# The first block's output projection in plain fp32, other buffers for the query chunks and the first gathered rows, and a new place for four steps of dot products

## The chip, the cores and the metric

The kernel runs on one core of a Trainium2 chip. The metric is the device time of one execution, in microseconds (us); the times given are the median of three runs and their lowest and highest. The profile is one execution, and its span is counted from the first to the last instruction. The engines are PE (matmuls; PEld is its weight load), DVE (vector), ACT (scalar activations), POOL (which issues the gathers here) and SP (which issues the plain loads). All of them run their own programs in order and wait for each other by semaphores.

## What is computed

A transformer block with a mixer (pooling and attention) and a PEER feed-forward layer, and behind it a second block (two kinds of attention, and a convolutional feed-forward layer). 256 tokens, width 1024, fp32. What the change touches is in the first block:

```
mod = c_act @ w_ada[l] + b_ada[l]
shift1, scale1, gate1, shift2, scale2, gate2 = jnp.split(mod, 6, axis=-1)
h = modulate(x, norm_mix_g[l], shift1, scale1)
proj = h @ w_in[l]
...
merged = g_pool * (pooled @ w_branch_pool[l]) + g_attn * (attn @ w_branch_attn[l])
x = x + gate1[:, None, :] * (merged @ w_out[l])
h2 = modulate(x, norm_ffn_g[l], shift2, scale2)
x = x + gate2[:, None, :] * peer_ffn(h2, peer_wq[l], peer_sub_keys[l], peer_u[l], peer_v[l])
```

`peer_ffn` picks, for each token and each of 8 heads, 16 of 16384 experts. The scores are `h2 @ w_q` against 2 x 128 keys per head; two rounds of top 16 give the indices. Each chosen expert has a row of 1024 numbers for a dot product with h2 and a row of 1024 numbers to be added with the weight `softmax * gelu(dot)`. That is 2 x 128 rows for each tile of 128 tokens, 256 gathers in all, of 128 x 2048 numbers (1 MiB) each.

## The kernel before

**Memory.** `ring` holds six slots of 128 x 4096 numbers. Slots 0 to 3 take weight chunks of 2 MiB; slots 4 and 5 of the ring hold eight "high parts" (below) of 128 x 1024 numbers. The chunk table also knows slots 4 and 5 for chunks, which are the first two 4096 columns of `util`; `util` holds the gates of the mixer in its columns 0 to 4095, `merged` in 4096 to 6143, and a low part (`lo_r`) in 6144 to 8191. In the gather stage every ring slot is two row buffers, named (slot, half).

**Split matmuls.** Most weights are used in two parts of a reduced fp32 format: ACT writes the high part (`split_high`, L498), DVE the rest (`split_low`, L873), in quarters of a chunk, and PE makes three passes (high x high, high x low, low x high). The output projection (`mixed`, L1630) does so too: 4 groups (2 tiles of tokens x 2 halves of the columns) of 8 x 3 matmuls of 128 x 512. For it ACT also splits `merged` (`xm high`, L639) and DVE its rest (L1069). A few matmuls, such as those with the gathered rows (L1761), are in plain fp32; each then stands in the trace as two instructions.

**The mixer.** SP loads the chunks in the order of `chunk_table`, each when what was in its slot has been read; a load that waits holds up all behind it. `ada` chunks are not used by PE: DVE multiplies the four parts of a chunk with a row and sums them (`ada(c)`, L884, 4 instructions of 128 x 1024), and the chunk's slot (slot 1 for the late ones) is free for the next `ada` chunk when that is done. The attention runs in a loop of 11 steps on PE, ACT and DVE alike. In a step i PE does the scores of head i (L1473), two quarters of the input projection (L1421, 48 matmuls), the turning of the probabilities of head i - 2 (L1481), the values of head i - 3 (L1492, L1493) and small pieces of the pooling branch (L1593, L1594, L1602); from step 7 it does `branch(0, z)` (L1572) in place of the input projection. DVE does the masks of head i (L931), the norms of head i - 1 (L915, L918), low parts, and in steps 0, 1, 3 and 5 `ada(8)` to `ada(11)`; in step 6 also the low parts of the pooling branch (`xp low`, L896), for which `branch(0, 0)` waits. ACT does the exponentials of head i behind the mask of head i.

**From the mixer to the gathers.** PE: `branch(1, z)`, then `mixed` for (tile 0, half 0), (0, 1), (1, 0), the turned rows of tile 0 (L1516), the queries and scores of head 0 for tile 0 (L1662, L1672), `mixed(1, 1)` (L1630), head 1's queries and tile 1's. DVE: `merge` of each quarter (L1065, L1067), the residual of each projected half (L962, L965), and the routing of head 0 in tile 0, in whose midst stands the residual of (tile 1, half 1). The routing ends with the indices (L1165), for which POOL waits to issue the first gather.

**The gathers.** `FIRST_BUFS` names the seven row buffers that are used first; `LATER_BUFS` adds five more at given rows, when the query chunks have been read. A buffer is free when PE has added its last row (event `rows`). Of two rows (later four, at the end one) DVE takes the dot products (L1237), ACT the gelu (L733) and the diagonals (L738), PE adds the rows (L1761). PE does the other queries in pieces between the rows (L1647). After the last row SP loads the second block's first chunks.

## Time and profile before

| | us |
|---|---|
| median of 3 runs (lowest to highest) | 1257.58 (1256.51 to 1258.30) |
| the profiled execution, its own time | 1258.39 |
| its span | 1256.6 |
| PE busy in the span | 1094.6 |
| DVE busy | 834.0 |
| ACT busy | 438.4 |
| DMA engines, q0 (gathers), share of the span | 51.5% |
| DMA engines, q1 (plain loads), share of the span | 24.6% |

The span falls into the mixer and projection (0 to about 231 us), the gathers (to about 890 us) and the second block. A row of a timeline gives the start, the length of the group of instructions, the engine, the line, what is written and read, the count, and in brackets how long the engine had been idle before and what ended that. Times between two rows are differences of their starts. PEclk is the granted clock of PE, where 1.00 is 2.4 GHz and 0.50 is 1.2 GHz.

### The profile page before, as it was taken

To read this page: it belongs to the slowest core of one execution; us is meant where nothing else is said; L and a number is where in the kernel's file an instruction comes from. 1 tells how busy PE (TensorE), PEld (TensorE's weight loads), DVE (VectorE), ACT (ScalarE), POOL (GpSimd) and SP (SyncE) were. 2 spreads that over 40 slices of the span, in tenths; PEclk is the share of its full clock that TensorE was granted. 3 is DMA by queue.
4 is the path that set the end of the run, shared out by engine and by line. 5 is a ranking of instruction groups with operands and counts; after the bars stand their busy time and mean duration, and the time that the engine had idled before them with its cause. 6 is when DMAs were issued, how large, how long until landed. Compare 5 with 4: busy or idle time off the path is not lost.

```text
span 1256.6 us, 13533 instructions
## 1 busy us (share of the span) xinstructions
PE 1094.6 (87%) x4970; PEld 734.5 (58%) x4970; DVE 834.0 (66%) x1903; ACT 438.4 (35%) x908; POOL 289.8 (23%) x260
## 2 busy tenths in 40 slices
PE   5998899699899986876887878878799989999997
PEld 3797787554454442332333333333498768999986
DVE  5696675667777778778888454545645455887753
ACT  3533373232323232212223111112535454666542
POOL 0000000235445343443554544543000000000000
PEclk8999899899999999988898998989899998999999
DMA  9977531899999999999999999999653412545540
GB/s 376 427 299 308 204 119 68 348 398 412 422 421 421 421 422 421 422 421 421 418 422 421 421 421 421 422 420 422 253 225 135 168 44 91 178 191 202 185 151 34
DMA packets 47878, 389.39 MB, mean 310 GB/s; under 512 B 5442, under 2 KB 5826, under 8 KB 7236
## 3 DMA queue, kind: packets, MB, share of 16 engines
q0 software_dynamic: 36864, 268.45, 51.5%
q1 hardware_dynamic: 10948, 120.07, 24.6%
q8 instruction: 40, 0.66, 0.2%
q14 instruction: 26, 0.21, 0.0%
HBM read 387.45 MB, written 1.05 MB: 309 GB/s over the span
## 4 chain that ended last, share of the span: by engine, by line
PE 49%; DMA 29%; DVE 15%; ACT 4%; issue 1%; POOL 1%; SPq 1%; DVEq 0%; POOLq 0%
DMA ring<-in_uv,idx 23%; PE ps L1761 16%; PE ps L1421 14%; DMA ring<-in_w_ada 5%; PE ps L1886 5%; DVE ring L1237 3%; DVE ring_r L873 2%; DVE ring L884 2%; PE ps L1817 2%; PE ps L1443 2%; PE ps L1473 2%; PE ps L1647 1%; PE ps L1630 1%; PE ps L1572 1%; POOL ring L482 1%
## 5 line engine op out<-in xcount | busy, mean ns | idle before, releaser
L1761 PE MATMUL ps<-ring,probT 128*128 128x512 f32 x1024 | 499.2, 634 | 112.6 <-ACT probT L738 112.5
L1237 DVE CUSTOM_DVE_ANT_0 ring<-h2t,ring 128x1024 f32<-128x1024 f32 x256 | 310.1, 1223 | 179.7 <-DMA ring<-in_uv,idx 179.1
L482 POOL DMA_INDIRECT ring<-in_uv,idx x256 | 289.6, 1131 | 580.5 <-PE ps L1761 315.5
L1761 PEld LDWEIGHTS ps<-ring,probT 128*128 128x128 f32 x1024 | 200.7, 202 | 360.3 <-issue 202.7
L1421 PE MATMUL ps<-util_r,ring_r 128*128 128x256 f32 x1312 | 220.9, 287 | 5.1 <-DVE util_r L1209 3.9
L873 DVE TENSOR_TENSOR ring_r<-ring,ring_r 128x1024 fp32r<-128x1024 f32 x142 | 167.8, 1220 | 58.2 <-ACT ring_r L498 58.2
L1421 PEld LDWEIGHTS ps<-util_r,ring_r 128*128 128x128 f32 x1312 | 185.4, 193 | 10.2 <-issue 7.1
L498 ACT ACTIVATE ring_r<-ring 128x1024 fp32r<-128x1024 f32 x142 | 143.0, 1049 | 49.4 <-DMA ring<-in_w_in 26.3
L733 ACT ACTIVATE prob<-prob 128x2 f32<-128x2 f32 (+2 forms) x94 | 19.2, 204 | 381.0 <-DVE prob L1237 380.7
L1421 PE MATMUL ps<-h_r,ring_r 128*128 128x256 f32 x704 | 125.4, 281 | 0.0
L738 ACT ACTIVATE probT<-ct,prob 128x128 f32<-128x128 f32 x256 | 85.1, 392 | 73.9 <-DVE prob L1243 73.7
L1421 PEld LDWEIGHTS ps<-h_r,ring_r 128*128 128x128 f32 x704 | 108.2, 189 | 0.1
L884 DVE CUSTOM_DVE_ANT_0 ring<-h2t,ring 128x1024 f32<-128x1024 f32 x44 | 51.3, 1221 | 19.8 <-DMA ring<-in_w_ada 19.4
L1886 PE MATMUL ps<-ring_r,util_r 128*128 128x512 f32 x176 | 50.1, 395 | 0.0
L508 ACT ACTIVATE prob<-prob,mx 128x128 f32<-128x128 f32 (+1 forms) x48 | 21.5, 448 | 59.9 <-DVE mx L931 59.9
L1647 PEld LDWEIGHTS ps<-h_sb,ring 128*128 128x128 f32 x128 | 24.8, 195 | 24.8 <-issue 24.0
L1886 PEld LDWEIGHTS ps<-ring_r,util_r 128*128 128x128 f32 x176 | 32.9, 187 | 8.0
L1647 PE MATMUL ps<-h_sb,ring 128*128 128x256 f32 x128 | 36.5, 386 | 0.0
L1443 PE MATMUL ps<-ring_r,util_r 128*128 128x256 f32 x288 | 34.9, 281 | 0.0
L1443 PEld LDWEIGHTS ps<-ring_r,util_r 128*128 128x128 f32 x288 | 34.1, 188 | 0.7 <-issue 0.7
L1572 PE MATMUL ps<-area_r,ring_r 128*128 128x256 f32 x192 | 26.0, 298 | 5.3 <-DVE area_r L896 3.9
L1243 DVE TENSOR_TENSOR prob<-prob 128x2 f32<-128x2 f32 (+2 forms) x94 | 14.5, 155 | 23.6 <-ACT prob L733 23.6
(213 smaller groups left out, 1037.8 us busy)
## 6 DMA issues: line engine op xcount, KB each, us to landing
ring<-in_w_in SPq DMA_DIRECT2D x13, 2048.0 KB, 12.3
ring<-in_w_up SPq DMA_DIRECT2D x11, 2048.0 KB, 7.7
ring<-in_w_ada SPq DMA_DIRECT2D x7, 2048.0 KB
ring<-in_w_down SPq DMA_DIRECT2D x6, 2048.0 KB, 7.8
ring<-in_w_ada SPq DMA_DIRECT2D x8, 1024.0 KB, 15.5
ring<-in_w_out SPq DMA_DIRECT2D x4, 2048.0 KB, 8.5
ring<-in_w_q SPq DMA_DIRECT2D x3, 2048.0 KB, 7.6
ring<-in_w_br SPq DMA_DIRECT2D x2, 2048.0 KB, 10.0
```

Of the source, the lines that this page charges most:

```text
L482: e.indirect_dma_start(out=row_buf[n], out_offset=None, in_=uv, in_offset=bass.IndirectOffsetOnAxis(ap=idx[:, tt, k:k + 1], axis=0)).then_inc(
L498: e.activation(hi, w, ACT.Copy).then_inc(*high.put(q))
L738: e.activation(diag[:, n % 8, :], ident, ACT.Copy, scale=wt[:, tt, n % 128:n % 128 + 1]).then_inc(*acted.put(("diag", n)))
L873: e.tensor_tensor(lo, w, hi.bitcast(F32), ALU.subtract).then_inc(*low.put(q))
L884: e.tensor_tensor_reduce(wv, crow, wv, 1.0, 0.0, ALU.mult, ALU.add, mod[:, 4 * c + j:4 * c + j + 1]).then_inc(*made.put(("ada", c, j)))
L1237: e.tensor_tensor_reduce(u, h2t[:, tt, :], u, 1.0, 0.0, ALU.mult, ALU.add, av[:, tt, n % 128:n % 128 + 1]).then_inc(*made.put(("dot", n)))
L1421: ins = e.matmul(o[:, jj * T:(jj + 1) * T], w[:, k, :], r[:, k, :], start=(k == 0 and n == 0), stop=(k == KD - 1 and n == 2))
L1443: ins = e.matmul(o, r[:, k, tt * P:(tt + 1) * P], w[:, k, :, :], start=(k == 0 and n == 0), stop=(k == KD - 1 and n == 2))
L1572: ins = e.matmul(o[:, jj * T:(jj + 1) * T], w[:, k, jj * P:(jj + 1) * P], x3[:, k, :], start=(jj == 0 and k == 0 and n == 0), stop=(jj == ...
L1647: ins = e.matmul(bank(("q", h))[:, jj * T:(jj + 1) * T], w[:, k, z * P:(z + 1) * P], h_sb[:, k, :], start=(k == 0), stop=(k == KD - 1))
L1761: ins = e.matmul(acc[half][:, :], diag[:, n % 8, :], row_buf[n][:, D + half * 512:D + (half + 1) * 512], start=(k == 0), stop=(k == 127))
L1886: ins = e.matmul(ps[where["down", tt, half]][:, :], h[:, k, tile[tt]], w[:, 0, HALF[half]], start=(k == 0 and n == 0), stop=(k == KF - 1 a ...
```

## The change

1. **Projection.** `mixed` reads `merged` and the chunks `out` as they are: 8 plain fp32 matmuls of 128 x 512 in a group where there were 24 of the split kind. The eight `split_high` and `split_low` of the `out` chunks and the four splits of `merged` (L639, L1069) are gone.
2. **Query chunks.** Chunk q1 loads into ring slot 4 and q2 into ring slot 5 (the buffers of high parts; new slot numbers 6 and 7), q3 into the lower part of `util`, where the gates were. In SP's queue q1 now stands ahead of q0. q1 waits for quarter 35 (the last of `branch(0, z)`), q2 for quarter 39 (the last of `branch(1, z)`), q3 for the last `merge`. Before, q1, q2 and q3 waited for projections, q1 and q3 for the last, with q2 behind q1 in the queue.
3. **Row buffers.** The first seven are halves of slots 0, 2, 1 and 3, and slots 4 and 5 come in later, at the same rows. The very last row buffers are now those of slot 4, not of slot 1. The scores lie in the upper part of `util`; the splitting of tile 0's rows for the second block, which uses the same part, moves from row 156 to 196 on PE, and accordingly on ACT and DVE.
4. **Dot products.** `ada(8)` to `ada(11)` stand in steps 0, 2, 4 and 6, and the sum with the bias (`mod2`) in step 7.

```
@@ -52,7 +52,7 @@
              ("in", 6, 3), ("ada", 8, 1), ("br", 0, 0), ("ada", 9, 1), ("in", 7, 2), ("ada", 10, 1), ("br", 1, 3),
-             ("ada", 11, 1), ("out", 0, 2), ("out", 1, 1), ("keys", 0, 0), ("q", 0, 3), ("q", 1, 1), ("q", 2, 2), ("q", 3, 5)]
+             ("ada", 11, 1), ("out", 0, 2), ("out", 1, 1), ("keys", 0, 0), ("q", 1, 6), ("q", 0, 3), ("q", 2, 7), ("q", 3, 4)]
     then = ([("in2", i) for i in range(6)] + [("out2", 0), ("out2", 1)]
@@ -67,8 +67,8 @@
 Q2 = QUARTER["in2", 0, 0]
-FIRST_BUFS = ((4, 0), (4, 1), (0, 1), (5, 0), (5, 1), (3, 0), (3, 1))
-LATER_BUFS = {26: ((1, 0), 3), 27: ((1, 1), 3), 58: ((2, 0), 5), 59: ((2, 1), 5), 93: ((0, 0), 7)}
+FIRST_BUFS = ((0, 1), (2, 0), (2, 1), (1, 0), (1, 1), (3, 0), (3, 1))
+LATER_BUFS = {26: ((4, 0), 3), 27: ((4, 1), 3), 58: ((5, 0), 5), 59: ((5, 1), 5), 93: ((0, 0), 7)}
 BATCHES = [(n, 2) for n in range(0, 96, 2)] + [(n, 4) for n in range(96, 248, 4)] + [(n, 1) for n in range(248, 256)]
@@ -252,6 +252,7 @@
         slots = [ring[:, i * SLOT:(i + 1) * SLOT] for i in range(NW)] + [util[:, 0:SLOT], util[:, SLOT:2 * SLOT]]
+        slots += [ring[:, i * SLOT:(i + 1) * SLOT] for i in (4, 5)]
         slots_r = [ring_r[:, i * SLOT:(i + 1) * SLOT] for i in range(NW)] + [util_r[:, 0:SLOT], util_r[:, SLOT:2 * SLOT]]
@@ -284,11 +285,10 @@
         merged = three(util, 4096, 8)
-        xm_hi = area_r[:, 2048:4096].rearrange("p (k t) -> p k t", k=KD)
         rope_of = {"q": (qT, yT), "k": (kT, small[:, :].rearrange("p (j t) -> p j t", j=4))}
...
         Q3 = area[:, 0:4096].rearrange("p (j t) -> p j t", j=16)
-        s_all = util[:, 0:4096].rearrange("p (z j n) -> p z j n", z=2, j=16)
+        s_all = util[:, 4096:8192].rearrange("p (z j n) -> p z j n", z=2, j=16)
         sidx = stat[:, 0:256].bitcast(U32)
@@ -331,7 +331,7 @@

-        loaded = [Mark(sem(f"s_chunk{i}"), 16) for i in range(NW + 2)]
+        loaded = [Mark(sem(f"s_chunk{i}"), 16) for i in range(NW + 4)]
         half_loaded = {n: Mark(sem(f"s_half{n[0]}{n[1]}"), 16) for n in (("ada", 0), ("ada", 2), ("in", 0), ("ada", 1), ("ada", 3))}
@@ -360,8 +360,6 @@
                 return ("tokens", 0, 1)
-            if kind == "out":
-                return ("mix1", 1, i)
             if (kind, i) in TOKEN_CHUNKS:
@@ -393,7 +391,7 @@
         beside_in = {0: (26, 27), 3: (28, 29), 4: (30, 31)}
-        beside_br = {5: (32, 33), 6: (34, 35), 7: (36, 37), 8: (38, 39), 9: (40,)}
+        beside_br = {5: (32, 33), 6: (34, 35), 7: (36, 37), 8: (38, 39), }
         beside1 = [("in", 4 + (u + 1) // 2, 2 * ((u + 1) % 2)) for u in range(7)]
@@ -405,8 +403,12 @@
                     sp.wait_ge(done, ("rows", last_rows[slot]))
+                elif (kind, i) == ("q", 1):
+                    sp.wait_ge(done, ("quarter", 35))
+                elif (kind, i) == ("q", 2):
+                    sp.wait_ge(done, ("quarter", 39))
                 elif (kind, i) == ("q", 3):
-                    sp.wait_ge(done, ("mix1", 1, 1))
+                    sp.wait_ge(made, ("merge", 3))
                 elif earlier:
@@ -478,7 +480,7 @@
                 else:
-                    pool.wait_ge(done, {4: ("mix1", 1, 0), 0: ("quarter", 35), 5: ("mix1", 1, 1)}[b[0]])
+                    pool.wait_ge(done, {0: ("quarter", 35), 2: ("mix1", 1, 0), 1: ("mix1", 1, 1)}[b[0]])
                 e.indirect_dma_start(out=row_buf[n], out_offset=None, in_=uv,
@@ -624,22 +626,13 @@
                         xy_high(k)
-            split_high(41, 42)
             xy_high(3)
-            split_high(43)
             sqrt_table(44)
...
                     *acted.put(("gate1", half)))
-            for z in range(4):
-                act.wait_ge(made, ("merge", z))
-                act.wait_ge(done, ("pv", 1, 7))
-                e.activation(xm_hi[:, 2 * z:2 * z + 2, :], merged[:, 2 * z:2 * z + 2, :], ACT.Copy).then_inc(
-                    *acted.put(("xm high", z)))
-                split_high(44 + z)
-
             def shifted(tt, k):
@@ -666,7 +659,7 @@
                 act.wait_ge(done, ("scores", h, tt))
-                e.activation(s_all[:, tt, 2 * h:2 * h + 2, :],
+                e.activation(s_all[:, 1 - tt, 2 * h:2 * h + 2, :],
                              bank(("scores", h, tt))[:, 0:T].rearrange("p (j n) -> p j n", j=2), ACT.Copy).then_inc(
@@ -723,7 +716,8 @@
                     row_root(3, 0)
-                if b0 == 164:
+                if b0 == 204:
+                    act.wait_ge(made, ("gw", 1, 7))
                     for half in range(2):
@@ -1038,13 +1032,13 @@
                 split_low(*beside_in.get(i, ()))
-                if i in (0, 1, 3, 5):
-                    ada({0: 8, 1: 9, 3: 10, 5: 11}[i])
                 if i == 10:
...
                     attended(1, i - 3)
-                if i == 6:
+                if i in (0, 2, 4, 6):
+                    ada(8 + i // 2)
+                if i == 7:
                     dve.wait_ge(made, ("ada", 11, 3))
@@ -1057,7 +1051,6 @@
             pool_gated(3)
-            split_low(*range(41, 44))
             for z in range(4):
@@ -1065,12 +1058,6 @@
                 e.tensor_tensor(m, m, g, ALU.add).then_inc(*made.put(("merge", z)))
-                dve.wait_ge(acted, ("xm high", z))
-                e.tensor_tensor(lo_r[:, 2 * z:2 * z + 2, :], m, xm_hi[:, 2 * z:2 * z + 2, :].bitcast(F32),
-                                ALU.subtract).then_inc(*made.put(("xm low", z)))
-                if z > 0:
-                    split_low(43 + z)
-            split_low(47)
             def shifted(tt):
@@ -1125,7 +1112,7 @@
                 dve.wait_ge(acted, ("scores", h0, tt) if h0 + nh <= 2 else ("scores", h0 + nh - 1))
-                yield from top16((*key, "s"), 2 * nh, sv, si, s_all[:, tt, 2 * h0:2 * (h0 + nh), :], z3)
+                yield from top16((*key, "s"), 2 * nh, sv, si, s_all[:, 1 - tt, 2 * h0:2 * (h0 + nh), :], z3)
                 dve.wait_ge(made, (*key, "s", "at2", 2 * nh - 1))
@@ -1226,7 +1213,7 @@
                     x3_again(0)
-                if b0 == 168:
+                if b0 == 208:
                     for half in range(2):
@@ -1618,17 +1605,13 @@
             def mixed(tt, half):
-                o = group(("mix1", tt, half))[:, :]
-                o4 = o.rearrange("p (q n) -> p q n", q=4)
-                a = NW * SLOT + (QUARTER["out", half, 0] % HI) * 1024
-                wh = ring_r[:, a:a + 4096].rearrange("p (q k n) -> p k q n", q=4, k=KD)
-                wl = slots_r[SLOT_OF["out", half]].rearrange("p (k n) -> p k n", k=KD)
-                wait_low(QUARTER["out", half, 3])
+
+                o = group(("mix1", tt, half))
+                w = slots[SLOT_OF["out", half]].rearrange("p (k n) -> p k n", k=KD)
+                pe.wait_ge(loaded[SLOT_OF["out", half]], ("out", half))
                 for k in range(KD):
-                    pe.wait_ge(made, ("xm low", k // 2))
-                    for n, (to, w, x3) in enumerate(((o4, wh, xm_hi), (o4, wh, lo_r), (o, wl, xm_hi))):
-                        ins = e.matmul(to, x3[:, k, tile[tt]], w[:, k], start=(k == 0 and n == 0),
-                                       stop=(k == KD - 1 and n == 2))
+                    pe.wait_ge(made, ("merge", k // 2))
+                    ins = e.matmul(o[:, :], merged[:, k, tile[tt]], w[:, k, :], start=(k == 0), stop=(k == KD - 1))
                 ins.then_inc(*done.put(("mix1", tt, half)))
@@ -1679,7 +1662,7 @@
                     for z in range(2):
-                        a = (2 * tt + z) * P
+                        a = (2 * (1 - tt) + z) * P
                         ins = e.matmul(o[:, a:a + P], Q3[:, 2 * h + z, tile[tt]], keys3[:, 2 * h + z, :], start=True,
@@ -1751,7 +1734,7 @@
                 tt, k = divmod(n, 128)
-                if n == 156:
+                if n == 196:
                     turned_x(3, 0)
```

DVE's queue in steps 1 and 2 of the attention loop; L931 (now L925) is the mask of a head, L915 and L918 (L909 and L912) are its norm, L884 (L878) is one of the four dot products of `ada(9)`. Before:

```order
L915 RECIPROCAL mx<-mx 128x2 [waits s_act]
L918 TENSOR_SCALAR prob<-prob,mx 128x128 [waits s_dve]
L918 TENSOR_SCALAR prob<-prob,mx 128x256
L884 ISA ring,mod<-h2t,ring 128x1024 [waits s_chunk1]
L884 ISA mod 128x1
```

After:

```order
L912 TENSOR_SCALAR prob<-prob,mx 128x256
L925 ISA prob,mx<-ps2,ct 128x128 [waits s_pe]
L925 ISA mx 128x1
L925 ISA prob,mx<-ps2,ct 128x256
L925 ISA mx 128x1
L909 RECIPROCAL mx<-mx 128x2 [waits s_act]
L912 TENSOR_SCALAR prob<-prob,mx 128x128 [waits s_dve]
L912 TENSOR_SCALAR prob<-prob,mx 128x256
L878 ISA ring,mod<-h2t,ring 128x1024 [waits s_chunk1]
```

The mask and the norm of the next head now stand ahead of the wait for the chunk, not behind it.

DVE's queue between the branches and the projection; L1065 and L1067 (now L1058 and L1060) are a `merge`, L1069 is the low part of `merged`, L873 a low part of an `out` chunk. Before:

```order
L873 TENSOR_TENSOR ring_r<-ring,ring_r 128x8x128 [waits s_high] x3
L1065 TENSOR_TENSOR util<-ps1,util 128x512 [waits s_pe]
L1067 TENSOR_TENSOR util<-util 128x512 [waits s_dve]
L1069 TENSOR_TENSOR util_r<-util,area_r 128x512 [waits s_act]
L1065 TENSOR_TENSOR util<-ps4,util 128x512 [waits s_pe]
L1067 TENSOR_TENSOR util<-util 128x512 [waits s_dve]
L1069 TENSOR_TENSOR util_r<-util,area_r 128x512 [waits s_act]
L873 TENSOR_TENSOR ring_r<-ring,ring_r 128x8x128 [waits s_high]
```

After:

```order
L1058 TENSOR_TENSOR util<-ps1,util 128x512 [waits s_pe]
L1060 TENSOR_TENSOR util<-util 128x512 [waits s_dve]
L1058 TENSOR_TENSOR util<-ps4,util 128x512 [waits s_pe]
L1060 TENSOR_TENSOR util<-util 128x512 [waits s_dve]
L1058 TENSOR_TENSOR util<-ps2,util 128x512 [waits s_pe]
```

Only the merges are left, and none of them waits for ACT.

SP's queue at the end of the mixer; in_w_out are the `out` chunks, in_keysT the keys, in_w_q the query chunks. Before:

```order
L413 DMA ring<-in_w_out 128x4096 [waits s_dve]
L413 DMA ring<-in_keysT 128x2048 [waits s_pe]
L413 DMA ring<-in_w_q 128x4096 [waits s_pe] x2
L413 DMA ring<-in_w_q 128x4096
L413 DMA util<-in_w_q 128x4096
```

After:

```order
L415 DMA ring<-in_w_out 128x4096 [waits s_dve]
L415 DMA ring<-in_keysT 128x2048 [waits s_pe]
L415 DMA ring<-in_w_q 128x4096
L415 DMA ring<-in_w_q 128x4096 [waits s_pe]
L415 DMA ring<-in_w_q 128x4096
L415 DMA util<-in_w_q 128x4096 [waits s_dve]
```

The first query chunk behind the keys is now q1 and has no wait left of its own; the next is q0, which waits for PE as before; q2 follows it without another wait, and q3 waits for DVE's last merge, no longer for PE's last projection.

## Rows read from the trace of the kernel before

**Rows 1.** The page, section 4: the chain that ended last, its shares by line.

```profile
DMA ring<-in_uv,idx 23%; PE ps L1761 16%; PE ps L1421 14%; DMA ring<-in_w_ada 5%; PE ps L1886 5%; DVE ring L1237 3%; DVE ring_r L873 2%; DVE ring L884 2%; PE ps L1817 2%; PE ps L1443 2%; PE ps L1473 2%; PE ps L1647 1%; PE ps L1630 1%; PE ps L1572 1%; POOL ring L482 1%
```

**Rows 2.** Stretches of the trace: busy us of each engine, PEclk, DMA share, GB/s.

```profile
200.00:210.00 10.00, 9.88 (x42) 7.98 (x43) 3.32 (x8) 1.74 (x5) 0.00 (x0) 1.00 0.01 2
...
500.00:600.00 100.00, 78.45 (x157) 32.00 (x158) 81.72 (x233) 22.91 (x64) 42.41 (x37) 0.90 1.01 421
```

**Rows 3.** Timeline of PE in the attention loop (columns as told above).

```profile
111.17 5.94 PE L1421 MATMUL ps<-util_r,ring_r 128*128 128x256 f32 x48
121.78 0.88 PE L1481 MATMUL ps<-ct,prob 128*128 128x128 f32 x3 [4.67 <-ACT prob L508]
...
128.06 7.45 PE L1421 MATMUL ps<-util_r,ring_r 128*128 128x256 f32 x48
...
138.04 5.95 PE L1421 MATMUL ps<-util_r,ring_r 128*128 128x256 f32 x48
...
145.89 5.94 PE L1421 MATMUL ps<-util_r,ring_r 128*128 128x256 f32 x48
...
157.68 5.09 PE L1572 MATMUL ps<-area_r,ring_r 128*128 128x256 f32 x24 [3.87 <-DVE area_r L896]
```

**Rows 4.** Timeline of DVE in the same loop.

```profile
115.74 1.23 DVE L884 CUSTOM_DVE_ANT_0 ring<-h2t,ring 128x1024 f32<-128x1024 f32 x1 [7.33 <-DMA ring<-in_w_ada]
...
128.21 1.23 DVE L884 CUSTOM_DVE_ANT_0 ring<-h2t,ring 128x1024 f32<-128x1024 f32 x1 [0.38 <-DMA ring<-in_w_ada]
...
148.41 1.23 DVE L884 CUSTOM_DVE_ANT_0 ring<-h2t,ring 128x1024 f32<-128x1024 f32 x1 [7.38 <-DMA ring<-in_w_ada]
...
157.12 1.42 DVE L896 TENSOR_TENSOR area_r<-area,area_r 128x256 fp32r<-128x256 f32 x4
```

**Rows 5.** Timeline of SP: the issue of plain loads.

```profile
120.44 0.33 SPq L413 DMA_DIRECT2D ring<-in_w_ada  x1
135.54 0.33 SPq L413 DMA_DIRECT2D ring<-in_w_br  x1
135.91 0.62 SPq L413 DMA_DIRECT2D ring<-in_w_ada  x1
...
224.75 0.43 SPq L413 DMA_DIRECT2D util<-in_w_q  x1
```

**Rows 6.** Timeline of PE, the first and the next piece behind three projected groups.

```profile
190.76 0.39 PE L1630 MATMUL ps<-ring_r,area_r 128*128 128x512 f32 x1
...
211.43 1.95 PE L1516 MATMUL ps<-prob,x_sb 128*128 128x128 f32 x16
```

**Rows 7.** The chain in order of time: start, us, what.

```profile
218.27 5.62 PE ps L1630 x24
...
278.35 1.72 PE ps L1761 x4
```

**Rows 8.** Timeline of POOL: the issue of gather 0 and of gather 11.

```profile
231.09 1.07 POOL L482 DMA_INDIRECT ring<-in_uv,idx  x1 [230.64 <-DVE idx L1165]
...
264.40 0.94 POOL L482 DMA_INDIRECT ring<-in_uv,idx  x1 [1.68 <-PE ps L1761]
```

**Rows 9.** Timeline of DVE: dot products of rows 1, 11 and 255.

```profile
246.73 1.23 DVE L1237 CUSTOM_DVE_ANT_0 ring<-h2t,ring 128x1024 f32<-128x1024 f32 x1 [2.30 <-DMA ring<-in_uv,idx]
...
271.98 1.23 DVE L1237 CUSTOM_DVE_ANT_0 ring<-h2t,ring 128x1024 f32<-128x1024 f32 x1 [1.25 <-DMA ring<-in_uv,idx]
...
888.13 1.23 DVE L1237 CUSTOM_DVE_ANT_0 ring<-h2t,ring 128x1024 f32<-128x1024 f32 x1 [0.80 <-DMA ring<-in_uv,idx]
```

**Rows 10.** Timeline of SP behind the last row: the second block's first loads.

```profile
892.34 2.04 SPq L413 DMA_DIRECT2D ring<-in_w_in  x4
```

**Rows 11.** Timeline of ACT: the first high parts of the second block.

```profile
900.20 2.00 ACT L498 ACTIVATE ring_r<-ring 128x1024 fp32r<-128x1024 f32 x2 [4.87 <-DMA ring<-in_w_in]
```

**Rows 12.** Timeline of PE at the same place.

```profile
895.96 3.68 PE L1747 MATMUL ps<-prob,area 128*128 128x128 f32 x16 [3.70 <-DVE mx L989]
903.56 8.66 PE L1421 MATMUL ps<-util_r,ring_r 128*128 128x256 f32 x48 [3.92 <-DVE util_r L1209]
```

## The prediction, made before the changed kernel had run

> **What bounds the kernel now.** I read the page's chain first. Its largest share, 23% of the span, is the landing of gathered rows [rows 1]. The table of stretches then shows which limit that is: from 500 to 600 us the DMA engines are full (1.01) and move 421 GB/s [rows 2]. 256 gathers of 1.05 MB are 268.4 MB, or 637 us at that rate, 2.49 each, more than any engine needs for a row. So the gather stage can hardly get shorter. The kernel ends at (issue of gather 0) + (what the DMA moves ahead of it) + 637 and stalls + (what follows the last row). I therefore read three places in the timelines: the way to gather 0, issued at 231.09 [rows 8], the first landings, and the way from the last dot product, 888.13 [rows 9], to the second block's first column at 903.56 [rows 12].
>
> On the way to gather 0 PE stands still twice: 4.67 us to 121.78 and 3.87 to 157.68 [rows 3]. Both times DVE had waited in a step's dot products for their chunk, 7.33 and 7.38 us [rows 4], with the next head's mask or the low parts of the pooling branch behind it. While the projection runs (200 to 210) the DMA is idle, share 0.01 [rows 2]; three query chunks of 2.1 MB go out only at its end, the last at 224.75 [rows 5], right ahead of gather 0.
>
> **The change, term by term.** The profiled execution took 1258.39, 0.8 above the median of the runs; I sum against it and take the same difference off the median. Times in the attention loop are before's scale.
>
> *Dot products.* `ada(9)` moves behind mask and norm of head 2, whose inputs are there. DVE then does them at 108.4 and waits for the same chunk to 115.74 as before, but PE has what it needs. Its column of step 3 ends at 111.17 + 5.9 = 117.1, and the 4.67 of waiting goes. So does the slow stretch behind it: the pieces from 121.78 to 128.06 took 6.3, and the 48 matmuls took 7.45 against 5.95 at full clock [rows 3], so 3.1 + 1.5 more. The next column starts at 117.1 + 3.2 = 120.3. From 128.06 to 138.04 is 10.0, less the 1.5 that the slow matmuls cost, 8.5: the column of step 5 starts at 128.8, that of step 6, 7.85 later (138.04 to 145.89), at 136.7. That is 9.2 ahead. DVE's low parts for steps 5 and 6 are done by my replay of the two queues at about 125 and 130, ahead of PE.
>
> `ada(10)` now starts behind the low parts of step 4, at 130.7 (its chunk, 7.8 on the way, landed at 128.21 [rows 4, 5]), and ends at 135.4. Then `ada(11)`'s chunk is issued, hardly earlier than before (135.91). But the `br` chunk that SP issued 0.4 ahead of it [rows 5] waited for PE's column of step 4 and now goes at 126.2; alone the `ada` chunk takes 7.8, not 12.5, and lands at 143.2. DVE reaches it behind the copy of head 3's values, at 142.6 (end of PE's column) and 1.5 for pieces and copy, 144.1. Four instructions of 1.23 [rows 4] end at 149.0 at the latest; PE's first branch starts 0.56 behind the start of L896 (157.68 and 157.12), at 149.5 instead of 157.68: **8.2 earlier**. The stall of 4 us stays, now behind `ada(11)` itself. Everything to the end of the branches follows PE at the same distance. `mod2` one step later delays nobody: its reader on PE is 20 us off.
>
> *Projection.* Before, the first three groups run from 190.76 to 211.43, 20.7 us [rows 6], though one such group alone takes 5.62 [rows 7]: 3.8 are waits for splits. In plain fp32 a group is 16 instructions; four such, with the same 128 x 512 shape, take 1.72 [rows 7], so 6.88 a group and 20.6 for three: **0.0**. The merges cover it: the last is ready about 1.5 behind the start, and its columns are read 5 behind it. The fourth group costs 6.88 - 5.62 = **1.2**, and DVE waits for it in the midst of the routing, ahead of the indices. The dropped splits on ACT and DVE had been the cause of those 3.8 and are worth nothing more.
>
> The trace shows 16 fp32 instructions at 6.88 against 24 split ones at 5.62, a factor of 1.22 [rows 7]. The Trainium skill, in FP8 and Floating Point Precision, section TensorE Precision Notes, counts four passes for a true fp32 matmul; against three for the split form this would be 4/3, an estimate of 7.5 a group, and 4.0 us on the path in place of 1.2. The row has the same shape in fp32, so I go by the row.
>
> *Query chunks.* q1 goes out when quarter 35 is done and q0, q2 and q3 at the end of the branches; all have landed 20 us before gather 0, in DMA time that was empty. PE's fp32 queries find q0 as before. SP has no other load behind them that matters. In before, gather 1 was used at 246.73; less 2.49 that is a first landing of 244.24, 13.15 behind the issue at 231.09 [rows 8, 9]. With an empty DMA it is at least 6.2: 1.07 on POOL, 2.49 of transfer, and what a lone chunk has beyond its transfer, 7.8 - 2.1/0.421 = 2.8, if 0.2 of this overlaps. It is at most 7.6, which gather 11 took with two others on the way, from 264.40 to 271.98 [rows 8, 9]. I take 6.6, near the lower end, since nothing is in front of it: **6.5 earlier** (5.5 to 6.9). Then the seven buffers cycle as before: row 0's end follows from the landing of row 1 in both, so the same 2.6 us behind, and the stalls until the sixth pair of buffers comes in are the same. PE, the pacer here, is as late relative to the landings.
>
> The Trainium skill, in DMA: Bandwidth & Descriptors, section Anatomy of one DMA, fits 2.0 us + bytes/436 GB/s to a DMA from GpSimd. For a gather that is an estimate of 4.4, and the sum would be 2.2 us lower. No row of before shows a gather that short.
>
> *After the last row.* The loads of the second block went out at 892.34, when PE had added row 255 in slot 1 [rows 10]; the first landed at 900.20 [rows 11] and its split let PE go at 903.56. Now slot 1's last row is 253, so SP is held by the landing of row 255 alone, 888.1. The chunk lands at 896.0, the split is done at 898.6 and the turned rows on PE, which end at 895.96 + 3.68 = 899.6 [rows 12], are last. PE goes on at 899.7: **3.9 earlier**, and the stall of 3.92 is gone. Its 48 matmuls took 8.66 there against 5.95 [rows 3, 12]; without the idle time up to 2.7 of that go. I take **1.5**, about the middle, since PE starts this place at the low clock anyhow.
>
> *Moved and hidden.* The split of tile 0's rows from row 156 to 196 (8 matmuls, two copies, two subtractions) stays beside a full DMA and is needed only after row 255; its new wait, for the last weights of the routing, was over some 30 rows before. Were it not hidden it would cost 3 us.
>
> Sum: 8.2 - 1.2 + 6.5 + 3.9 + 1.5 = 18.9. 1258.39 - 18.9 = 1239.5 for a profiled execution, **1238.7** for the median.
>
> **The rivals.** *The forecast*, 1235 to 1243, with each term within its bounds.
>
> *A stall in place of the one removed.* If `ada(11)`'s chunk lands no earlier than 148.41, the branches start at 148.4 + 4.9 + 0.6 = 153.9, 3.8 earlier and not 8.2: 1243.1. For it: its issue hardly moves. Against: the `br` chunk is out of its way by 9 us.
>
> *Buffers.* The DMA is empty sooner, and seven buffers do not keep it full if PE begins row 0 at half clock and stays there for three rows more; each costs 1.7 then: about 5 us, 1243.7. For it: PE idles ahead of row 0 in both. Against: it did so before too, for longer.
>
> *Slower.* The fp32 projection at 1.2 GHz. PE's stall ahead of the branches stays, and the granted clock has been down behind such stalls. Four groups at half clock take 27.5 more, which the merges can't hide: 1238.7 + 27.5 = 1266.2. It decides from where more than 70% of the projection runs at the low level (18.9 of 27.5). Against: the clock is 1.00 there now, 30 us behind the stall [rows 2], and PE has no gap between.
>
> *It doesn't do what it says.* If gathers were held by something other than the loads (the landing stays 13 us behind the issue) and the chunk behind the last row by the DMA, 10 us of the sum would go: 1249.
>
> **How the numbers follow.** Forecast 0.70, stall 0.12, buffers 0.09, not what it says 0.05 (0.01 of it with no gain that could be told), slower 0.03, faster than all of this 0.01. The likeliest is 1238.7. The range goes from 1234, all terms at their ends and the first landing still earlier, to 1247, stall and buffers together. It leaves out the last three. A difference under 0.2% (2.5 us) can't be told from none. Faster by more 0.96, within 0.01, slower by more 0.03.
>
> **What would show it.** Right: no idle PE between 117 and 121; an idle of 4 to 5 us ahead of the first branch, at 149 to 150; the last query chunk issued near 184; gather 0 issued near 224 and the first dot product within 8 us of it; the last dot product near 875; the second block's loads issued within 1 us of it, and no second wait of PE ahead of the first column. Wrong: three groups of the projection over 22 us; a DMA share under 0.95 anywhere in the first 60 us of the gathers for more than before; a first landing more than 9 us behind its issue.

## The result

The changed kernel takes **1240.18 us** (median of 4 runs, 1238.98 to 1245.5), the kernel before 1257.94 beside it (4 runs, 1256.51 to 1260.88). The ratio is 0.9864, 95% interval 0.983 to 0.9898: 12.8 to 21.4 us faster. 1238.7 was forecast, 1234 to 1247 as the range. The profiled execution took 1240.34, with a span of 1238.4.

The page of the changed kernel: its head and the chain by engine and by line, as [rows 1].

```profile
span 1238.4 us, 13445 instructions
...
PE 52%; DMA 29%; DVE 12%; ACT 4%; issue 1%; POOL 1%; SPq 0%; DVEq 0%; POOLq 0%
DMA ring<-in_uv,idx 25%; PE ps L1408 16%; PE ps L1744 16%; PE ps L1869 5%; DMA ring<-in_w_ada 4%; DVE ring L1224 3%; PE ps L1614 2%; PE ps L1800 2%; PE ps L1559 2%; PE ps L1460 2%; PE ps L1430 2%; DVE ring_r L867 2%; DVE ring L878 2%; PE ps L1630 1%; POOL ring L484 1%
```

The gathers are still the largest item and their stage has not become shorter; what lies ahead of it and behind it has. In the timelines below a row is: start, us, engine, line, operation, out and in, count, and in brackets the idle time ahead of it and what ended it. PE of the changed kernel in the attention loop, as [rows 3]:

```profile
110.62 5.95 PE L1408 MATMUL ps<-util_r,ring_r 128*128 128x256 f32 x48
119.76 5.95 PE L1408 MATMUL ps<-util_r,ring_r 128*128 128x256 f32 x48
128.24 5.95 PE L1408 MATMUL ps<-util_r,ring_r 128*128 128x256 f32 x48
136.09 5.95 PE L1408 MATMUL ps<-util_r,ring_r 128*128 128x256 f32 x48
...
148.68 5.46 PE L1559 MATMUL ps<-area_r,ring_r 128*128 128x256 f32 x24 [4.67 <-DVE area_r L890]
```

No idle time near 117, every column at full speed, and the second stall still there, with another cause. DVE shows which: the four instructions of `ada(11)` start at 143.54 and wait for no chunk, the low parts follow at 148.12.

```profile
143.54 1.21 DVE L878 CUSTOM_DVE_ANT_0 ring<-h2t,ring 128x1024 f32<-128x1024 f32 x1
...
148.12 1.42 DVE L890 TENSOR_TENSOR area_r<-area,area_r 128x256 fp32r<-128x256 f32 x4
```

The projection on PE (as [rows 6, 7]), the last query chunk on SP (as [rows 5]), gather 0 on POOL and the dot product of row 1 on DVE (as [rows 8, 9]):

```profile
182.17 20.76 PE L1614 MATMUL ps<-ring,util 128*128 128x512 f32 x48
...
209.44 7.03 PE L1614 MATMUL ps<-ring,util 128*128 128x512 f32 x16
...
183.81 0.33 SPq L415 DMA_DIRECT2D util<-in_w_q  x1
...
223.70 1.07 POOL L484 DMA_INDIRECT ring<-in_uv,idx  x1 [223.25 <-DVE idx L1152]
...
232.87 1.22 DVE L1224 CUSTOM_DVE_ANT_0 ring<-h2t,ring 128x1024 f32<-128x1024 f32 x1 [2.38 <-DMA ring<-in_uv,idx]
```

And the way out of the gathers, SP and PE (as [rows 10, 12]). The last dot product starts at 873.68, and SP no longer waits for PE:

```profile
873.67 2.06 SPq L415 DMA_DIRECT2D ring<-in_w_in  x4
...
881.51 3.48 PE L1730 MATMUL ps<-prob,area 128*128 128x128 f32 x16 [3.70 <-DVE mx L983]
885.09 5.92 PE L1408 MATMUL ps<-util_r,ring_r 128*128 128x256 f32 x48
890.86 2.90 PE L1777 MATMUL ps<-util_r,small_r 128*8 128x256 f32 x24
```

**Where 18.2 us of span went.** The execution is cut into pieces at the same instructions in both kernels. Both kernels were traced a second time (`before_again`, `after_again`, below), on two different chips; the last column is that pair. Each forecast is a term of the prediction's sum. Minus is time saved.

| piece | forecast | first pair | second pair |
|---|---|---|---|
| start to the column of step 2 | 0 | -0.55 | -0.50 |
| to the first branch (dot products) | -8.2 | -8.45 | -5.99 |
| to the start of the projection | 0 | +0.41 | -0.74 |
| to gather 0 (plain fp32) | +1.2 | +1.20 | +1.20 |
| to the dot product of row 1 (query chunks) | -6.5 | -6.47 | -6.67 |
| to the dot product of row 255 | 0 | -0.59 | +0.79 |
| to the second block's first column | -3.9 | -4.02 | -4.20 |
| its 48 matmuls (clock) | -1.5 | -2.73 | -1.00 |
| to the end | 0 | +3.00 | -0.79 |
| sum | -18.9 | -18.20 | -17.90 |

The last piece of the first pair is the surprise: 3.0 us of what had been won is given back some 100 us behind the change. The two rows are stretches of the changed kernel in the attention of the second block (busy us of PE, PEld, DVE, ACT, POOL, then PEclk, DMA share, GB/s):

```profile
988.00:992.00 4.00, 3.50 (x11) 2.17 (x11) 2.43 (x9) 2.87 (x8) 0.00 (x0) 0.50 0.00 0
992.00:996.00 4.00, 4.00 (x10) 2.81 (x9) 2.73 (x9) 2.81 (x8) 0.00 (x0) 0.50 0.02 4
```

PE runs at the lower of its two levels (1.2 GHz) there, behind several short waits (0.4 to 0.8 us each, from 982 on). Whether the change did that, or chance, is asked below, under `after_again`.

### The profile page after: what moved, and what is told of

Same layout as the page of the kernel before. It is cut to its first block, busy times and chain, and to the rows that moved or that the text cites. A ratio compares the mean times of both kernels' runs of the same rounds, so it can differ in the third digit from the quotient of the medians.

```text
span 1238.4 us, 13445 instructions
## 1 busy us (share of the span) xinstructions
PE 1092.4 (88%) x4938; PEld 723.5 (58%) x4938; DVE 821.9 (66%) x1891; ACT 428.2 (35%) x896; POOL 292.4 (24%) x260
## 4 chain that ended last, share of the span: by engine, by line
PE 52%; DMA 29%; DVE 12%; ACT 4%; issue 1%; POOL 1%; SPq 0%; DVEq 0%; POOLq 0%
DMA ring<-in_uv,idx 25%; PE ps L1408 16%; PE ps L1744 16%; PE ps L1869 5%; DMA ring<-in_w_ada 4%; DVE ring L1224 3%; PE ps L1614 2%; PE ps L1800 2%; PE ps L1559 2%; PE ps L1460 2%; PE ps L1430 2%; DVE ring_r L867 2%; DVE ring L878 2%; PE ps L1630 1%; POOL ring L484 1%
## 5 line engine op out<-in xcount | busy, mean ns | idle before, releaser
L1408 PE MATMUL ps<-util_r,ring_r 128*128 128x256 f32 x1312 | 216.6, 282 | 2.3 <-DVE ring_r L867 2.2
L867 DVE TENSOR_TENSOR ring_r<-ring,ring_r 128x1024 fp32r<-128x1024 f32 x134 | 158.3, 1220 | 54.7 <-ACT ring_r L500 54.7
L1408 PEld LDWEIGHTS ps<-util_r,ring_r 128*128 128x128 f32 x1312 | 181.0, 188 | 7.0 <-issue 3.9
L500 ACT ACTIVATE ring_r<-ring 128x1024 fp32r<-128x1024 f32 x134 | 134.6, 1049 | 46.5 <-DMA ring<-in_w_in 23.4
L878 DVE CUSTOM_DVE_ANT_0 ring<-h2t,ring 128x1024 f32<-128x1024 f32 x44 | 51.2, 1219 | 9.6 <-DMA ring<-in_w_ada 9.4
```

The costliest lines, as they stand in the source:

```text
L500: e.activation(hi, w, ACT.Copy).then_inc(*high.put(q))
L867: e.tensor_tensor(lo, w, hi.bitcast(F32), ALU.subtract).then_inc(*low.put(q))
L878: e.tensor_tensor_reduce(wv, crow, wv, 1.0, 0.0, ALU.mult, ALU.add, mod[:, 4 * c + j:4 * c + j + 1]).then_inc(*made.put(("ada", c, j)))
L1408: ins = e.matmul(o[:, jj * T:(jj + 1) * T], w[:, k, :], r[:, k, :], start=(k == 0 and n == 0), stop=(k == KD - 1 and n == 2))
```

## The experiments

Eleven runs were made: eight edited kernels, one of them twice, and the two kernels of the comparison once more each. Times are medians with the ratio to the kernel before, which ran beside them, and its 95% interval. They fall into three groups, each on a chip of its own: `e1` to `e4`, with 1257.65 for the kernel before (20 runs); `e5`, `e6`, `e7` and `after_again`, with 1258.31 (7); `e7_again`, `e8` and `before_again`, with 1257.04 (9).

### Dot products alone (`e1`)

The kernel before, with this edit on DVE:

```
-                if i in (0, 1, 3, 5):
-                    ada({0: 8, 1: 9, 3: 10, 5: 11}[i])
...
+                if i in (0, 2, 4, 6):
+                    ada(8 + i // 2)
-                if i == 6:
+                if i == 7:
```

> The kernel before with one edit: ada(8) to ada(11) in steps 0, 2, 4 and 6, the sum with the bias in step 7. Theory (the dot products on DVE hold PE, and all that follows moves with PE): the idle of 4.67 us ahead of 121.78 goes, the first branch on PE starts near 149 instead of 157.68, gather 0 is issued near 223 instead of 231.09, and the median falls by 8.2 from 1257.9 to 1249.7. Rival (the gain needs the other parts, because the splits of the output weights or the query chunks then set gather 0): gather 0 stays within 3 us of 231.09, the median is above 1255. The tail behind the last row is untouched in both: 3.9 of idle ahead of the second block's first column.

Measured: 1252.12 us (10 runs), 0.9959 (0.994 to 0.9978). PE and POOL of this kernel:

```profile
148.90 5.46 PE L1572 MATMUL ps<-area_r,ring_r 128*128 128x256 f32 x24 [4.68 <-DVE area_r L896]
...
222.78 1.07 POOL L482 DMA_INDIRECT ring<-in_uv,idx  x1 [222.34 <-DVE idx L1165]
```

Both landmarks are where the theory put them (149, 223), so the gain needs no other part of the change. But by the ratio the time fell by 5.2 (2.8 to 7.5), not by 8.2. From the column of step 2 to the first branch this trace takes 46.18; the kernel before took 54.65 in its first trace, but the kernel of `e2`, whose loop is before's, took 52.44. The second trace of before, further down, shows what differs.

### Plain projection alone (`e2`)

The kernel before, with `mixed` as in the changed kernel and the splits for it gone:

```
-            split_high(41, 42)
...
-            split_high(43)
...
-                act.wait_ge(made, ("merge", z))
...
-            split_low(*range(41, 44))
...
-                dve.wait_ge(acted, ("xm high", z))
...
-                    pe.wait_ge(made, ("xm low", k // 2))
+                    pe.wait_ge(made, ("merge", k // 2))
+                    ins = e.matmul(o[:, :], merged[:, k, tile[tt]], w[:, k, :], start=(k == 0), stop=(k == KD - 1))
```

> The kernel before with one edit: the projection in plain fp32 from the unsplit chunks, no splits of them and none of merged. Theory (a plain group costs 1.25 more than a split one on PE, the 3.8 of waits in the first three groups covered that): three groups in 20.6 us, the fourth in 6.9, the median 1.2 up, 1259.1. Rival (the splits on ACT and DVE were a cost of their own, which goes): gather 0 earlier than 231.09 by up to 3.8, the median 1254 to 1257.

Measured: 1261.31 us (10 runs), 1.0023 (1.0006 to 1.004). PE and POOL:

```profile
189.43 20.76 PE L1612 MATMUL ps<-ring,util 128*128 128x512 f32 x48
...
216.70 7.03 PE L1612 MATMUL ps<-ring,util 128*128 128x512 f32 x16
...
230.95 1.07 POOL L482 DMA_INDIRECT ring<-in_uv,idx  x1 [230.50 <-DVE idx L1150]
```

From the start of the projection to gather 0 it is 41.52 us; before 231.09 - 190.76 = 40.33, and 40.32 with the dot products moved alone. So plain fp32 costs **1.20 us** on the way to gather 0, and the many splits that it saves on ACT and DVE are worth nothing there. The time rose by more, 2.9 by the ratio, but the interval (0.8 to 5.0) holds the 1.20. In the trace the landing of row 1 (0.8) and the second block's first column (1.1) come later too, and the mean granted clock of the ten executions is 0.944, against 0.950 in the twenty of before. Whether plain fp32 brings any of that, no run shows. By itself this part of the change is a loss; it pays by what it frees, the buffers of the high parts, into which the query chunks can go early.

### Query chunks late (`e3`)

The changed kernel, with q0 first in SP's queue again and the others behind the last projected group:

```
-             ("ada", 11, 1), ("out", 0, 2), ("out", 1, 1), ("keys", 0, 0), ("q", 1, 6), ("q", 0, 3), ("q", 2, 7), ("q", 3, 4)]
+             ("ada", 11, 1), ("out", 0, 2), ("out", 1, 1), ("keys", 0, 0), ("q", 0, 3), ("q", 1, 6), ("q", 2, 7), ("q", 3, 4)]
...
                 elif (kind, i) == ("q", 1):
-                    sp.wait_ge(done, ("quarter", 35))
-                elif (kind, i) == ("q", 2):
-                    sp.wait_ge(done, ("quarter", 39))
-                elif (kind, i) == ("q", 3):
-                    sp.wait_ge(made, ("merge", 3))
+                    sp.wait_ge(done, ("mix1", 1, 1))
```

> The changed kernel with one edit: q1, q2 and q3 go out only when the last projected group is done, into their new buffers. Theory (6.3 MB of query chunks ahead of the first gathers is what delayed the first landing in before): gather 0 is issued as in the changed kernel, near 223.7; row 1's dot product starts 15 us behind the issue instead of 9.2, and the median is 6.5 up, 1246.7. Rival (the first landing depends on something else, the buffers' places or the clock): row 1's dot product within 10 us of the issue, the median 1240 to 1242.

Measured: 1247.21 us (5 runs), 0.9925 (0.99 to 0.9951), 7.0 above the changed kernel. The dot products of rows 0 and 1, behind a gather 0 issued at 223.01:

```profile
235.62 1.23 DVE L1220 CUSTOM_DVE_ANT_0 ring<-h2t,ring 128x1024 f32<-128x1024 f32 x1 [7.33 <-DMA ring<-in_uv,idx]
...
239.56 1.23 DVE L1220 CUSTOM_DVE_ANT_0 ring<-h2t,ring 128x1024 f32<-128x1024 f32 x1 [2.70 <-DMA ring<-in_uv,idx]
```

Row 1 comes 16.55 behind the issue, against 9.17 in the changed kernel, and row 255 is 7.7 later (881.35 against 873.68). The queue of chunks ahead of the first gather is the cause of that part.

### Second loads late (`e4`)

The changed kernel, with one more wait of SP ahead of the second block's loads:

```
             sp.wait_ge(arrived[255], 255)
+            sp.wait_ge(done, ("rows", 255))
```

> The changed kernel with one edit: SP sends the second block's loads only when PE has added row 255, as before the change. Both theories: the loads go out 4.2 later, near 877.9, PE waits a second time ahead of the first column and runs it at the low clock (8.7 instead of 5.9 us), so the 24 matmuls behind it start 6.6 later. Theory 1 (the cost of the tail is paid to the end): the median is 6.6 up, 1246.8. Theory 2 (the half-clock stretches of the attention behind it, at 988 to 997 and 1035 to 1041, are there because this one is missing; they cost 4.2 us more than before's, of which 1.2 comes back at 1042): they shrink again and 3.0 of the 6.6 comes back, 1243.8.

Measured: 1245.17 us (4 runs), 0.991 (0.9878 to 0.9942), 5.0 above the changed kernel. SP and PE:

```profile
878.34 1.97 SPq L415 DMA_DIRECT2D ring<-in_w_in  x4
...
889.39 8.60 PE L1409 MATMUL ps<-util_r,ring_r 128*128 128x256 f32 x48 [3.86 <-DVE util_r L1197]
897.82 2.96 PE L1778 MATMUL ps<-util_r,small_r 128*8 128x256 f32 x24
```

The second wait and the slow column are back, and the median lies between those of the two theories. Set to the last dot product, the 24 matmuls start 23.70 behind it (897.82 - 874.12) and 17.18 in the changed kernel: 6.5 us, as both theories said. Against the first trace of the changed kernel these matmuls start 6.96 later (897.82 - 890.86), and at the end of the span only 4.0 us of that remain, which is what theory 2 said. But this is no proof of it, as the next run shows.

### The changed kernel once more (`after_again`)

> The changed kernel once more, unedited, on this chip, for a second trace. Theory (from the first matmuls of the second block to the end of its attention an execution takes 143.4 us, or 2.3 to 3.3 more where the granted clock falls in the attention; which of the two, no kernel decides): this stretch, from the 24 matmuls behind the first column to the second LayerNorm's rows, is at 143.4 or between 145.5 and 147. Rival (the change itself brings the fall of the clock at 988 to 997, since the earlier one behind the first column is gone): it is above 145.5 again. The landmarks up to the last dot product repeat within 0.7 us of the first trace. Median 1240 to 1242.

Measured: 1240.35 us (4 runs), 0.9861 (0.9839 to 0.9884). The landmarks repeat less well than expected: row 255 is within 0.3 us, but gather 0 (222.74) is 1.0 and row 1 (231.74) 1.1 earlier than in the first trace. From the 24 matmuls to the second LayerNorm's rows it took 144.42 us, where the first trace has 146.70: neither at 143.4 nor between 145.5 and 147, so the two levels that the theory named are not two. From the 24 matmuls to the end of the span the thirteen traces have 344.5 to 347.5. The kernels with the long wait in the tail have 344.5 and 346.5 (before), 346.5 (`e1`), 347.3 (`e2`) and 344.6 (`e4`); those without it 347.5 and 345.7 (the changed kernel), 344.6 (`e3`), 346.9, 345.4, 345.4, 347.5 and 344.6 (`e5` to `e8`). The spread inside either group is as wide as that between them. That the change brings the fall of the clock is not borne out; that 3 us come and go there from one execution to the next is.

### The kernel before once more (`before_again`)

> The kernel before once more, for a second trace of its attention loop. Theory (after PE's idle of 4.67 us at 121.78 the granted clock falls in some executions only, and in those the loop is 2.2 us longer): either as in the first trace, 48 matmuls at 128.06 in 7.45 us and the first branch at 157.7, or as in e2_plain_alone, 5.94 us and the first branch at 155.5. Rival (the clock falls there always, and e2's earlier branch has another cause): 7.45 and 157.7 again.

Measured: 1256.8 us (one run). PE in the attention loop, as [rows 3]:

```profile
121.47 0.87 PE L1481 MATMUL ps<-ct,prob 128*128 128x128 f32 x3 [4.74 <-ACT prob L508]
...
127.11 5.95 PE L1421 MATMUL ps<-util_r,ring_r 128*128 128x256 f32 x48
...
154.82 5.46 PE L1572 MATMUL ps<-area_r,ring_r 128*128 128x256 f32 x24 [3.47 <-DVE area_r L896]
```

The same stall as in the first trace, but the branch 2.86 earlier (2.48 set to the column of step 2). The stretches behind the stall, first of the first trace, then of this one (PEclk is the third number from the end):

```profile
121.00:125.00 4.00, 3.22 (x9) 2.08 (x10) 1.77 (x10) 4.00 (x14) 0.00 (x0) 0.53 0.91 291
125.00:129.00 4.00, 4.00 (x13) 2.63 (x12) 3.15 (x3) 2.41 (x5) 0.00 (x0) 0.50 0.55 233
129.00:133.00 4.00, 4.00 (x27) 4.00 (x26) 4.00 (x9) 0.00 (x0) 0.00 (x0) 0.69 0.01 2
```

```profile
121.00:125.00 4.00, 3.53 (x11) 2.33 (x12) 1.50 (x9) 4.00 (x12) 0.00 (x0) 0.50 1.00 348
125.00:129.00 4.00, 4.00 (x24) 3.02 (x24) 3.49 (x3) 2.10 (x5) 0.00 (x0) 0.83 0.41 176
129.00:133.00 4.00, 4.00 (x36) 4.00 (x35) 4.00 (x11) 0.20 (x1) 0.00 (x0) 1.00 0.03 6
```

So the theory needs mending: the clock falls behind the stall both times (0.53, 0.50), and what differs is how soon it is back, by some 5 us: a clock of 0.69 from 129 to 133 means the low level to about 131.5, one of 0.83 from 125 to 129 means to about 126.4. The dot products are worth 8.45 against the one trace and 5.99 against the other. `e1`'s 5.2 fits the second better, and `e2`'s loop, 52.44, was of the short kind too (52.17 here). That the short kind is the usual one, three traces don't show.

### The last dot products later (`e5`)

The changed kernel, with `ada(11)` one step later:

```
-                if i in (0, 2, 4, 6):
-                    ada(8 + i // 2)
+                if i in (0, 2, 4, 7):
+                    ada(8 + min(i, 6) // 2)
```

> The changed kernel with one edit: ada(11) in step 7, behind the mask and norm of head 7, and no longer in step 6 ahead of the low parts of the pooling branch. Theory (the 4.67 us for which PE stands ahead of its first branch are the four dot products of ada(11) alone, nothing is late behind them): the low parts start at 143.5 instead of 148.1, the first branch near 144.1 instead of 148.7, and it runs at full clock (3.1 instead of 5.5 us), since PE has not stood still: 4.6 to 6.9 earlier, median 1240.2 - 5.5 = 1234.7. Rival (another wait takes the place: the second output chunk, which is released later, or the splits of step 7 behind ada(11)): the projection starts less than 2 us earlier, median 1238 to 1242.

Measured: 1236.4 us (4 runs), 0.9835 (0.9807 to 0.9863). PE and POOL:

```profile
144.06 3.08 PE L1559 MATMUL ps<-area_r,ring_r 128*128 128x256 f32 x24
...
218.21 1.07 POOL L484 DMA_INDIRECT ring<-in_uv,idx  x1 [217.77 <-DVE idx L1152]
```

PE does not stand still at all ahead of its first branch, which also runs at full clock. Gather 0 is 5.5 earlier, row 255 6.0 (867.66), the median 3.8, less than the 4.6 to 6.9 that were expected. The stall that the prediction left in place "behind `ada(11)` itself" was four instructions in the wrong place. A small part of it comes back at the fourth branch:

```profile
156.40 0.55 PE L1468 MATMUL ps<-ct,prob 128*128 128x128 f32 x3 [0.96 <-DVE prob L912]
...
159.60 3.10 PE L1559 MATMUL ps<-area_r,ring_r 128*128 128x256 f32 x24 [1.86 <-DVE util L933]
```

PE waits for DVE, which is now later by the four instructions, for 0.96 + 1.86 = 2.82 us in step 9 and 10, where the changed kernel has one wait of 1.47. Here the clock stayed up; in `e7` and `e8`, which have the same edit, it did not.

### The indices first (`e6`)

The changed kernel, with this edit on DVE:

```
-            advance(routing, 8)
+            advance(routing, 14)
             rows_added(2, 1, (1,))
-            advance(routing, 2)
             row_part(2, 1)
-            advance(routing, 1)
             row_diagonal(2, 1)
-            advance(routing, 3)
             shifted(1)
```

> The changed kernel with one edit on DVE: the second half of tile 1's residual, its row sums and its diagonal stand behind the cast to the indices of head 0, not ahead of it. Theory (what a slower fourth projected group costs, it costs because DVE waits for it ahead of the indices): the wait of 2.48 and 1.9 us of work leave the way, gather 0 goes out at 219.3 instead of 223.7, the last dot product is 4.4 earlier, and the median is 1235.8. Rival (PE and DVE take the rows up no earlier, since PE's queries and tile 1's rows come later, and few buffers stall the gathers): gather 0 early, but the last dot product less than 2 us earlier, median 1238.5 to 1241.

Measured: 1239.07 us (4 runs), 0.9855 (0.9831 to 0.9878), not to be told from the changed kernel. POOL shows gather 0 where the theory had it, 0.6 early, and then what ate it:

```profile
218.66 1.07 POOL L484 DMA_INDIRECT ring<-in_uv,idx  x1 [218.22 <-DVE idx L1152]
...
223.76 0.94 POOL L484 DMA_INDIRECT ring<-in_uv,idx  x1 [0.30 <-issue]
231.34 1.63 POOL L484 DMA_INDIRECT ring<-in_uv,idx  x1 [6.63 <-PE ps L1642]
```

Five gathers go out, the sixth waits 6.63 us for PE's queries of tile 1 (L1642), whose chunk holds its buffer; in the changed kernel they ended earlier and it waited for nothing (POOL issued it at 230.06, 6.4 behind gather 0). DVE takes up row 0 only at 229.80. Row 255 is at 871.95, 1.7 earlier. The rival's numbers came, and its mechanism with them: most of an early gather 0 is lost again if the rows are taken up no sooner and the buffers behind it come later. Which of the two costs how much, this run doesn't part.

### Both (`e7`), and a milder form (`e8`)

> The changed kernel with the edits of the two runs before it together. If both hold, they lie behind one another on the same way to gather 0 and add up: gather 0 near 213.5 to 214.7, the median 10 below the changed kernel, 1230.3. If one of them only moves a wait, the sum is that of the other alone, 1235.

Measured: 1233.39 us (4 runs), 0.9798 (0.9771 to 0.9825), gather 0 at 215.79, 1.1 later than expected at the latest. The fourth branch, at the low clock, takes 1.5 more than in `e5`, which covers that lateness:

```profile
159.91 4.58 PE L1556 MATMUL ps<-area_r,ring_r 128*128 128x256 f32 x24 [1.86 <-DVE util L933]
```

The median is 6.8 below the changed kernel's, not 10, and row 255, at 870.08, even comes behind `e5`'s 867.66: the two edits don't add up in full. The sixth gather again waits 6.63 us for PE's queries, and row 1 is 0.9 behind `e5`'s; the other 1.6 lie between row 1 and row 255, a stretch that differs by 1.9 us from trace to trace anyway (below). `e8` takes twelve routing steps ahead of the residual and leaves two behind it (`advance(routing, 12)`, then one ahead of `row_diagonal` and one behind).

> The kernel of e5 (ada(11) in step 7) with a milder form of e6's edit: twelve steps of the routing instead of eight ahead of the second half of tile 1's residual, so that they fill DVE's wait of 2.48 us for the fourth projected group, and the rest of that work still ahead of the indices. Theory (e6 lost its 4.4 us because tile 1's queries, whose end frees the buffers of gathers 5 and 6, came 1.8 later, and the five gathers ahead of them had all landed): here the queries end as in e5, gather 0 goes out 2.0 us earlier than in e5 (216.2), gathers 5 and 6 follow without a pause, and the last dot product is at 865.7, 2.0 earlier than e5's 867.66. Rival (any earlier gather 0 is lost again, since PE takes up row 0 no sooner): last dot product at 867 to 868.

Measured: 1234.59 us (5 runs), 0.9821 (0.979 to 0.9853). From the end of the third projected group to gather 0 it is 18.87 us and 20.94 in `e5`, 2.1 less where 2.0 were expected, and row 1 keeps them (27.78 against 29.94), though the sixth gather waits 2.02 us for PE's queries and doesn't follow without a pause. By row 255 only 0.4 is left (670.03 against 670.39). The absolute times are those of `e5` (gather 0 at 218.16), since the fourth branch ran at the low clock, as in `e7` (24 matmuls in 4.62 in place of 3.10 us), and the whole trace was 0.5 later from step 2 on; row 255 is at 869.32, later than either theory had it. That gather 0 and row 1 move is seen, that it is worth anything at the end is not.

> The kernel of e7 once more, to set it against e8 in the same rounds. By the last dot product it should lose: 870.08 in its first trace, against 865.7 expected of e8. The medians then differ by 4 us, 1237 against 1233. Rival (what e7 loses in the gathers comes back behind them, as its first median of 1233.4 beside e5's 1236.4 says): medians within 1.5 us.

Measured: 1234.09 us (5 runs), 0.9806 (0.978 to 0.9832), row 255 at 870.79, the fourth branch once more slow (4.64 us). The medians of `e7` and `e8` are within 0.5 us of one another, as the rival said; that its reason is the right one isn't shown. `e5`, `e7` and `e8` can't be ranked by these runs; their medians are 3.8 to 6.8 us below the changed kernel's, and `e7`'s nine runs (1230.71 to 1237.43) lie below all eight of the changed kernel (1238.98 to 1245.5). So do the four of `e5` (1233.55 to 1238.69), by less; of the five of `e8` one doesn't (1240.24).

## Why the prediction was right, and where it was not

**The bound.** That the gather stage itself would not move held: from row 1 to row 255 641.40 before, 640.81 after (641.47 and 642.26 in the second pair; 640.3 to 642.3 over the thirteen traces).

**Dot products.** The replay of the loop was right to 0.8 us: the columns were forecast at 120.3, 128.8 and 136.7 and came at 119.76, 128.24 and 136.09, the branch at 149.5 and came at 148.68; 0.55 of that the run was ahead already. The step that was wrong is the one that took the slow matmuls behind the stall, "3.1 + 1.5 more", as a fixed part of the stall's price. In the second trace of before about 2.5 us of it aren't there. The difference between two medians holds an average of such draws, and the prediction had only one. The 8.45 of the first pair is near the forecast because both rest on the same trace of before.

**Projection.** 20.6 us for three groups and 6.87 for the fourth, forecast 20.6 and 6.88; 1.20 of cost against 1.2. The price came from the four matmuls of the same shape [rows 7]. From the four passes that the Trainium skill, in FP8 and Floating Point Precision, section TensorE Precision Notes, counts for a true fp32 matmul, the prediction had made an estimate of 7.5 a group; the runs stand with the row, 6.9. (The 4.0 us on the path that it gave for this case are 3.7 by its own figures.)

**Query chunks.** 6.47 against 6.5. Row 0's dot product starts 5.56 behind the issue, 0.28 after DVE began to wait, so the estimate of 4.4 that the prediction worked out from the Trainium skill, DMA: Bandwidth & Descriptors, section Anatomy of one DMA, is too short counted from the start of POOL's instruction. Counted from its end, 224.77, the way is 4.49, which is near it. The prediction's 6.6 was for row 1's dot product less one transfer, 6.68 as measured.

**After the last row.** 4.02 and 4.20 against 3.9. The clock term, set at 1.5 "about the middle", measured 2.73 and 1.00 in the two pairs; over the thirteen traces the column takes 7.3 to 8.7 us behind the long wait (five traces, mean 7.95) and 5.9 to 7.0 without it (eight, mean 6.26), so it is worth 1.7.

**What was missing.** The sum, 18.9, is near the 18.2 of the first pair in part by luck: the tail's clock gave 1.2 more and the small pieces together 1.1, and the attention behind it took 3.0, a piece that the prediction didn't look at. The forecast of 1238.7 is 1.5 under the median. Taken by the runs, the parts are 5.2 (`e1`), 7.0 (`e3`) and 5.0 (`e4`), less 1.2 to 2.9 (`e2`): 14.3 to 16.0 of the 17.1 that the ratio gives, each with 2 us or more of doubt either way. The upper end of the range, 1247, was said to be stall and buffers together; by the prediction's own terms that is 1248.1. Of the rivals none came: gather 1 to gather 6 went out without a wait, the chunk of `ada(11)` landed ahead of its use, and the projection ran at full clock, 6.9 us a group.

**What would have been better.** The prediction named the remaining stall of 4 us and its cause and passed on. Had it asked what else could stand in that place, it would have found the 4.6 us by which the first branch comes earlier in `e5`.

## What to carry to other kernels

Price a stall's removal in two parts, the wait itself and the slow clock behind it, and give the second a range of its own: between two traces of one kernel it differed by 2.5 us. A part of a change that costs time by itself (here plain fp32, 1.2 us) can be right for the memory it frees; look at what can then be loaded earlier. And where DVE waits in the midst of a queue, look at which of the instructions behind the wait others need; moving the four of `ada(11)` by one step brought gather 0 forward by 5.5 us and the median by 3.8; the whole change behind the last row is worth 5.0 (`e4`).
